# Streamed weights stored as interleaved pairs of chunks and read with a step of two, and a 32-byte pad that moves the operands behind it to multiples of 64 bytes

## The reference

```python
for l in range(2):
    mod = silu(c) @ w_ada + b_ada                       # shifts, scales, gates
    h = rmsnorm(x, norm1_g) * (1 + sc1) + sh1
    z = h @ w_in                                        # 1024 -> 3340 columns
    ...                                                 # HGRN2 | RG-LRU | gated DeltaNet heads
    x = x + gt1 * (concat(oa, ob, oc) @ w_out)
    h = rmsnorm(x, norm2_g) * (1 + sc2) + sh2
    x = x + gt2 * peer(h, wq, k1, k2, u, v)
y = rmsnorm(x, final_norm_g)

def peer(h, wq, k1, k2, u, v):                          # u, v: 16384 x 1024
    q = h @ wq; ...                                     # top 16 of 16384 experts in each of 8 heads
    gw = softmax(sc)
    act = gelu(einsum('thkd,td->thk', u[idx], h))
    return einsum('thk,thkd->td', gw * act, v[idx])
```

## Time and profile before

| | us |
|---|---|
| median of 3 runs | 2350.78 |
| lowest, highest | 2343.35, 2357.78 |
| the profiled execution's own time | 2358.03 |
| its span in the profile | 2356.1 |

### The profile page before, as it was taken

One profiled execution on the slowest core, in us unless ns is written; L12 is line 12 of the kernel. 1 busy time (PEld: TensorE's weight loads), 2 busy tenths in 40 slices (PEclk: granted clock), 3 DMA queues, 4 the chain that ended last, 5 costly groups with the idle time before them and its releaser, 6 DMA issues. The chain is left out here.

```text
span 2356.1 us, 57811 instructions
## 1 busy us (share of the span) xinstructions
PE 2249.4 (95%) x20446; PEld 2085.2 (89%) x20478; DVE 1495.8 (63%) x3099; ACT 1271.2 (54%) x2439; POOL 1054.3 (45%) x960
## 2 busy tenths in 40 slices
PE   6979999999999999999989799999999999999998
PEld 4956779999998799999979377799999978999997
DVE  3756527963225968888666663499422287887885
ACT  3634215567557855555556431355765597555554
POOL 0021007874445746566300210288544474665661
PEclk9978899999999999999999789999999999999999
DMA  7462034555554179889644602355555533898993
GB/s 285 153 251 91 12 135 164 177 186 201 187 188 164 63 266 312 288 301 313 204 162 163 257 30 92 124 180 179 196 187 187 187 117 129 299 310 272 311 310 101
DMA packets 123814, 455.52 MB, mean 193 GB/s; under 512 B 13744, under 2 KB 14256, under 8 KB 122544
## 3 DMA queue, kind: packets, MB, share of 16 engines
q1 hardware_dynamic: 105264, 386.80, 46.4%
q0 software_dynamic: 18432, 67.12, 10.4%
HBM read 449.37 MB, written 4.49 MB: 193 GB/s over the span
## 5 line engine op out<-in xcount | busy, mean ns | idle before, releaser
L430 POOL TENSOR_TENSOR parts<-ring,parts 128x512 fp32r<-128x512 f32 x358 | 463.8, 1299 | 475.0 <-ACT parts L423 461.4
L423 ACT ACTIVATE parts<-ring 128x512 fp32r<-128x512 f32 x620 | 389.3, 632 | 348.4 <-PE ps_u L477 280.8
L473 PE MATMUL ps_u<-h_parts,parts 128*128 128x256 f32 x4096 | 563.0, 280 | 1.0 <-ACT parts L423 0.6
L2691 PE MATMUL ps_y<-act_parts,parts 128*128 128x256 f32 x4096 | 562.8, 279 | 0.0
L473 PEld LDWEIGHTS ps_u<-h_parts,parts 128*128 128x128 f32 x4096 | 514.4, 188 | 3.5 <-ACT parts L423 2.0
L2691 PEld LDWEIGHTS ps_y<-act_parts,parts 128*128 128x128 f32 x4096 | 515.1, 188 | 0.8 <-ACT parts L2631 0.7
L430 DVE TENSOR_TENSOR parts<-ring,parts 128x512 fp32r<-128x512 f32 x262 | 180.7, 693 | 372.0 <-ACT parts L423 350.5
L2740 POOL TENSOR_TENSOR act_parts<-big,act_parts 128x256 fp32r<-128x256 f32 x256 | 246.4, 962 | 303.5 <-ACT act_parts L2720 303.5
L477 PE MATMUL ps_u<-h_parts,parts 128*128 128x256 f32 x2048 | 322.2, 279 | 1.4 <-DVE parts L430 1.1
L2695 PE MATMUL ps_y<-act_parts,parts 128*128 128x256 f32 x2048 | 322.7, 279 | 0.0
L477 PEld LDWEIGHTS ps_u<-h_parts,parts 128*128 128x128 f32 x2048 | 275.4, 188 | 2.2 <-DVE parts L430 1.5
(11 more groups left out here) (407 smaller groups left out, 2801.3 us busy)
## 6 DMA issues: line engine op xcount, KB each, us to landing
ring<-in_stream SPq DMA_DIRECT2D x506, 512.0 KB, 3.5
more_ring<-in_stream SPq DMA_DIRECT2D x126, 512.0 KB, 5.1
extra_ring<-in_stream SPq DMA_DIRECT2D x32, 512.0 KB, 5.4
mod_ring<-in_stream SPq DMA_DIRECT2D x32, 512.0 KB, 3.3
big<-in_stream SPq DMA_DIRECT2D x16, 512.0 KB, 11.6
out_state_out<-big SPq DMA_DIRECT2D x2, 1440.0 KB, 6.9
big<-in_state SPq DMA_DIRECT2D x2, 1280.0 KB, 10.6
big<-in_mixc SPq DMA_DIRECT2D x2, 1024.0 KB, 8.1
```

What stands on the lines that cost most here:

```text
L423: eng.activation(m.parts[:, q % PARTS, 0, :], half_tile(m, t, half), ACT.Copy).then_inc(s["hi_ready"], 1)
L430: eng.tensor_tensor(m.parts[:, q % PARTS, 1, :], half_tile(m, t, half), m.parts[:, q % PARTS, 0, :].bitcast(F32), ALU.subtract).then_inc(m ...
L473: pe.matmul(out, hi[:, k, :], hr[:, side, kk, 0:tokens], start=(kk + side == 0), stop=False)
L2691: pe.matmul(ps[:, half * KD // 2 + k, :], hi[:, k, :], act_parts[:, j % AHEAD, side, :], start=False, stop=False)
```

## The change

Three things are changed, and no instruction is added, removed or moved in the program of any engine: the same instructions stand in the same order, and only the addresses and steps of their operands differ.

1. On the host, the tiles that go through the split, and so all of w_in, u and v (not the tiles of w_ada, the gates' tile, w_out and peer_wq), are stored with each two chunks of 128 columns interleaved: column n of chunk 2j at place 2n of the pair's 256, column n of chunk 2j + 1 at place 2n + 1.
2. `part` gives a list of chunks instead of one view. A chunk's 128 columns are then read as weights with a step of two elements (8 bytes), over 1024 bytes of the partition and not 512. ScalarE's, VectorE's and GpSimd's split still works on 512 columns in a row. Rows of v that are gathered from `stream` come interleaved too, so `m.tokens` is read with a step of two at line 2702 (2704 in the changed kernel).
3. A tensor `line_end` of 32 bytes that nothing uses stands behind `small`. Everything behind it moves by 32 bytes: `mod` ... `big` (63680), `x_parts`, `h_parts`, `onehot`, `act_parts` (210624) and `more_ring` (214720) now begin at multiples of 64 bytes. So do the moving operands of all float32r matmuls. The odd chunk of a pair begins 4 bytes behind such a multiple.

```diff
@@ Memory
         self.small = sb("small", [P, SMALL_W])
+        self.line_end = sb("line_end", [P, 8])
         self.mod = sb("mod", [P, 6 * KD, 1 + NB])
@@ part
-    return m.parts[:, q % PARTS, side, :].rearrange("p (k n) -> p k n", k=KD // 2)
+    pairs = m.parts[:, q % PARTS, side, :].rearrange("p (j n b) -> p j n b", j=KD // 4, b=2)
+    return [pairs[:, k // 2, :, k % 2] for k in range(KD // 2)]
@@ split_product (the same in combine_block's tile)
-                pe.matmul(out, hi[:, k, :], hr[:, side, kk, 0:tokens], start=(kk + side == 0), stop=False)
+                pe.matmul(out, hi[k], hr[:, side, kk, 0:tokens], start=(kk + side == 0), stop=False)
...
-            mm = pe.matmul(out, lo[:, k, :], hr[:, 0, kk, 0:tokens], start=False, stop=(kk == KD - 1))
+            mm = pe.matmul(out, lo[k], hr[:, 0, kk, 0:tokens], start=False, stop=(kk == KD - 1))
@@ combine_block
+            tokens = m.tokens.rearrange("p (j n b) -> p j n b", j=KD // 2, b=2)
             for k in range(KD):
-                mm = pe.matmul(ps_m[:, NSAMP * k:NSAMP * (k + 1)], m.tokens[:, k * P:(k + 1) * P], m.folded,
+                mm = pe.matmul(ps_m[:, NSAMP * k:NSAMP * (k + 1)], tokens[:, k // 2, :, k % 2], m.folded,
                                start=True, stop=True)
@@ host_layout
+    for tiles in (slice(T_BETA, T_LOCAL0), slice(T_U, T_X)):
+        chunks = stream[:, tiles].reshape(DEPTH, -1, P, KD // 2, 2, P)
+        stream[:, tiles] = chunks.transpose(0, 1, 2, 3, 5, 4).reshape(DEPTH, -1, P, D)
```

More of the change, by code:

```diff
@@ L2690, in tile @@
                         for k in range(KD // 2):
-                            pe.matmul(ps[:, half * KD // 2 + k, :], hi[:, k, :], act_parts[:, j % AHEAD, side, :],
+                            pe.matmul(ps[:, half * KD // 2 + k, :], hi[k], act_parts[:, j % AHEAD, side, :],
                                       start=False, stop=False)
@@ L2694, in tile @@
                     for k in range(KD // 2):
-                        mm = pe.matmul(ps[:, half * KD // 2 + k, :], lo[:, k, :], act_parts[:, j % AHEAD, 0, :],
+                        mm = pe.matmul(ps[:, half * KD // 2 + k, :], lo[k], act_parts[:, j % AHEAD, 0, :],
                                        start=False, stop=False)
```

## The result

The changed kernel takes 2391.15 us in the median of 3 runs (2384.44 to 2391.64), 40 us more than before: a ratio of 1.015, 95% interval [1.012, 1.018]. It is slower, by an interval that leaves out 1, where 2280 us was forecast and 2375 us was the upper end of the range.

A forecast was written before the change was run, and what follows sets the result against it. TensorE's back-to-back float32r matmuls were taken as the bound; 61 us (256 columns) plus 13 (288) gave 74, less 3 for waits, 71 us. From the median of 2350.8 that made 2280 us (-3.0%), range 2235 to 2375.

The forecast's parts named there:

- What bounds the kernel: Experts', combine and projection stages: TensorE starting float32r matmuls back to back, 1606 of the 2356 us.
- DMA, VectorE and the top-k: Work beside TensorE: DMA share 0.97, VectorE at 90%; waits beside the top-k cost about 1.5 us in each layer.
- the fold: Line 2702, `m.tokens` read with a step of two: counted as 0, or 3.6 us if its records took twice as long.
- 256 columns need 107 to 109 ns: Floor of moving columns for the split's matmuls, at 0.42 ns a column, against a measured interval of 116.7 ns.
- the sum: All float32r matmuls: intervals fall to 111.7 ns (256 columns) and 122.3 (288), saving 61 + 13 = 74 us.
- the excess: Interval above the higher floor, 4.7 ns with 256 columns and 10.7 with 288, taken as delayed reading.
- I take that it costs nothing by itself: Weights read with a step of two: the load keeps its 112 ns and the excess ends.
- if the step costs the load more than 5 ns: Sign that the forecast is wrong: the load had only 5 ns of slack in an interval of 116.7.
- The rival that came true: Weights' step makes it slower: the load's reads double the excess, 8 and 11 ns a matmul, 112 us, 2463 us; chance 0.15.
- Alone the pad seems to be worth nothing: Moving operands at multiples of 64: plain float32 intervals at 0 and 32 modulo 64 are 242.5 and 242.4 ns.
- The prediction's bounds for the pad with the step: Moving operands at multiples of 64 together with stepped weights: worth from 0 to the whole excess.
- Nothing changes: Rival: the excess is a property of float32r with the array full, not of addresses; 2351 us, chance 0.20.

The follow-up runs named there:

- moving_step2: Kernel before, combine cut to loads of 64 weights and 128 moving columns, read with step two, then contiguous: 115 and 62 ns a matmul at full clock.

## Why the prediction was wrong

- **What bounds the kernel** was right: these 13584 matmuls, one behind the other, with TensorE full and all else waiting. No wait that this had hidden came out; DMA, VectorE and the top-k played no part, and the fold cost 0.2 us.
- **The step that failed first is "256 columns need 107 to 109 ns".** It was read from plain float32 and bfloat16 rows and applied to float32r. A float32r stream takes 117.5 ns even beside a load of 32 weights, and 113.3 at the least beside full ones: 1.77 to 1.84 ns for the 16 bytes of every four columns. So of the 5.0 ns that the sum saves at each matmul 3.4 at most were there to save, in the 1360 period, which the change doesn't reach. The rows at hand said so: 116.7 / 64 and 132.7 / 72 are 1.82 and 1.84. I had noticed that the excess grows with the columns and took that for proof of interference, when it is just as well the mark of a dearer column.
- **"I take that it costs nothing by itself" failed next, and this is the step that made the kernel slower.** The step adds 6 ns to a load at the fold (112 to 118) and 8 in the split's form (112 to 120), measured beside 128 columns, which by moving_step2 need only some 60 ns. The load had been the lower floor, 112 beside columns of 113 to 118. With the step it is the higher one, and the interval is its 120.0 ns. No cost of load and columns to each other is needed for that, and none is seen. It met the prediction's own last sign of being wrong, "if the step costs the load more than 5 ns". Why 64 lines take 118 to 120 ns in a load, and not 64 x 1.8 = 115, stays open.
- **The rival that came true** is the slower one, in its direction and its point ("as soon as the mean interval is over 117 ns"), at about a third of its price: 3.3 ns and not 8, and none with 288 columns, where the columns' 132.7 stays above the load (without the pad these too took 1 ns more). Its reason failed: it let the load take its time from the moving columns, and the load itself became longer.
- **The pad.** "Alone the pad seems to be worth nothing" held for the time (1.002 [0.998, 1.005]), though not for the interval, which it moves: the difference of the addresses chooses the set of periods, 1400 and 1413 or 1413 and 1360. What moves an interval by 1 ns is too small for these times. The prediction's bounds for the pad with the step, from 0 to the whole excess, were too wide: it is worth 10 ns of 1450.
- **"Nothing changes"** leaned on a rule of the Trainium skill (TensorE: Matmul & The Clock Gate, section Step-by-step: what each phase is for): two independent read ports, so that a load takes nothing from the running matmul. The runs agree with that rule where they test it: at the same addresses the columns take 117.5 ns beside a quarter load and 116.7 beside a full one, and stepped full loads 120 beside 128 columns and beside 256. The rule doesn't give 0 for the sum, since a load can become longer by itself. That the periods depend on the difference of the two addresses shows that the two streams are not wholly free of each other; how they meet was not shown.

## What to carry to other kernels

Count the 16-byte lines that each operand of a matmul touches, beside its columns: here a line cost about 1.8 ns for the moving operand, and 1.8 to 1.9 for weights with a step of two to four, and a contiguous float32r moving operand is at that limit already. With 256 columns the load and the columns stand so close that 8 ns on the lower one turn the order round. Take a floor only from rows of the same data type and the same operand, and before a stall is blamed on interference, run it with each of the two partners made small, and look at the single intervals: a mean can hide a short first one. Where a stream keeps an exact period for hundreds of repeats, look for other periods in it: addresses and one short instruction ahead moved it by 3.8%, more than the change under study.

## What was not expected of the hardware

- Contiguous streams of float32r matmuls lock into one of several periods (1360, 1400, 1413, 1420, 1433, 1440, 1453 ns for 12), by the difference of the operands' addresses modulo 64 and by how the stream was started. Why a restart ends in 1590 or in 1637 ns, and so in 1360 or 1413, stays open.
- The price of a line is the same at either clock level: 128 float32r columns with a step of two, 64 lines, take 117 ns at 1.2 and at 2.4 GHz, where contiguous ones take 107 and 60.
- Interleaving in groups of four columns, where each line that is touched is used in full, was not tried, nor a step of more than four elements, which would tell lines from bytes.
